# Hybrid attention block on one core: the attention weights turned by VectorE and DMA instead of TensorE, with the maximum, the scaling, the key order and the start-up rearranged

## The reference, cut to what matters

```python
h = rms_norm(x, norm_w)                       # x: 512 x 2048, fp32
proj = h @ w_in                               # 2048 x 6144
q, k, v, g_a, u_p, g_p = split(proj)          # 1024 columns each
# per head (8 heads, two components c of 64 each): q, k normed, rotary on 16 of 64
s = einsum('bhcqd,bhckd->bhcqk', q, k) / 8    # 512 keys
p = softmax(s)
a = p[:, :, 0] - lam * p[:, :, 1]             # differential attention
o = einsum('bhqk,bhke->bhqe', a, v)           # v: 512 keys x 128
attn = rms_norm(o, subln_w) * 0.8
pool = centred means of u_p over windows 2, 4, 8, 16, minus u_p, @ w_pool
x = x + concat(attn * silu(g_a), pool * silu(g_p)) @ w_out   # 2048 x 2048
```

## Time and profile before

| what | value |
|---|---|
| median of 3 runs | 777.97 us |
| the profiled execution | 778.13 us, span 776.3 us |
| PE busy | 769.8 us (99%) |
| PEld busy | 637.0 us (82%) |
| DVE busy | 551.0 us (71%) |
| ACT busy | 381.6 us (49%) |
| POOL busy | 31.3 us (4%) |
| chain that ended last | PE 96% |
| granted TensorE clock | 1.000 |

### The profile page before, as it was taken

The page is one execution under the profiler, slowest core; times in us unless marked ns, Lnnn a source line. Parts: engine busy times, 40 slices in busy tenths (PEclk is TensorE's granted clock), DMA queues, the critical chain, the costliest instruction groups (busy, mean ns, idle before and its releaser), DMA issues.

```text
span 776.3 us, 9638 instructions
## 1 busy us (share of the span) xinstructions
PE 769.8 (99%) x3458; PEld 637.0 (82%) x3458; DVE 551.0 (71%) x861; ACT 381.6 (49%) x649; POOL 31.3 (4%) x42
## 2 busy tenths in 40 slices
PE   9999999999999999999999999999999999999997
PEld 8788888888888888888888888888888888888886
DVE  5543235888854788985478897348888869987796
ACT  5463134444474354455354355554345665655552
POOL 0010000000000000000000000000000003322200
PEclk9999999999999999999999999999999999999999
DMA  9853323452222354221234421224432169999972
GB/s 333 327 194 92 98 89 102 135 156 70 74 73 64 109 149 126 78 81 55 81 110 147 122 81 57 79 78 139 140 105 81 56 233 255 276 275 263 211 168 108
DMA packets 67079, 106.22 MB, mean 137 GB/s; under 512 B 5344, under 2 KB 46560, under 8 KB 66528
## 3 DMA queue, kind: packets, MB, share of 16 engines
q1 hardware_dynamic: 60288, 86.72, 34.6%
q0 software_dynamic: 4736, 16.78, 11.0%
q10 hardware_dynamic: 2016, 2.18, 0.9%
HBM read 95.17 MB, written 4.19 MB: 128 GB/s over the span
## 4 chain that ended last, share of the span: by engine, by line
PE 96%; SPq 2%; DMA 1%; issue 0%; DVE 0%; ACT 0%
PE ps L457 94%; PE ps L584 2%; DMA raw<-in_w_in 1%; SPq L329 1%; SPq L286 1%; SPq L293 0%; SPq L331 0%; PE ps L625 0%; DVE x_left L1213 0%; ACT w_hi L675 0%
## 5 line engine op out<-in xcount | busy, mean ns | idle before, releaser
L903 DVE TENSOR_TENSOR w_lo<-raw,w_hi 128x512 fp32r<-128x512 f32 x240 | 163.4, 689 | 166.3 <-ACT w_hi L685 90.8
L457 PE MATMUL ps<-h_hi,w_hi 128*128 128x512 f32 x640 | 251.0, 392 | 0.0
L457 PE MATMUL ps<-h_lo,w_hi 128*128 128x512 f32 x640 | 249.3, 390 | 0.0
L457 PE MATMUL ps<-h_hi,w_lo 128*128 128x512 f32 x640 | 171.2, 389 | 0.0
L685 ACT CAST w_hi<-raw 128x512 fp32r<-128x512 f32 x149 | 90.6, 621 | 156.2 <-PE ps L457 155.4
L457 PEld LDWEIGHTS ps<-h_hi,w_lo 128*128 128x128 f32 x640 | 120.1, 188 | 25.1
L457 PEld LDWEIGHTS ps<-h_hi,w_hi 128*128 128x128 f32 x640 | 120.2, 188 | 24.6
L457 PEld LDWEIGHTS ps<-h_lo,w_hi 128*128 128x128 f32 x640 | 120.2, 188 | 24.5
L457 PE MATMUL ps<-w_hi,h_hi 128*128 128x512 f32 x352 | 122.0, 391 | 1.5 <-ACT w_hi L675 1.5
L457 PE MATMUL ps<-w_hi,h_lo 128*128 128x512 f32 x352 | 121.4, 389 | 0.0
L457 PE MATMUL ps<-w_lo,h_hi 128*128 128x512 f32 x352 | 121.4, 389 | 0.0
(11 more groups left out here) (143 smaller groups left out, 785.4 us busy)
## 6 DMA issues: line engine op xcount, KB each, us to landing
raw<-in_w_in SPq DMA_DIRECT2D x96, 512.0 KB, 3.7
raw<-in_w_out SPq DMA_DIRECT2D x12, 512.0 KB, 3.8
raw<-in_w_out POOLq DMA_DIRECT2D x12, 512.0 KB, 17.0
wide_b<-in_w_out POOLq DMA_DIRECT2D x12, 512.0 KB, 18.7
x_rows<-in_x SPq DMA_DIRECT2D x4, 1024.0 KB, 12.8
tall<-in_w_out SPq DMA_DIRECT2D x8, 512.0 KB, 13.1
tall<-in_w_out POOLq DMA_DIRECT2D x8, 512.0 KB, 23.4
mixed<-in_x_cols SPq DMA_DIRECT2D x3, 1024.0 KB, 13.2
```

What stands on the lines that cost most here:

```text
L457: last = nc.tensor.matmul(dst, lhs, rhs, start=first and i == 0, stop=final and i == len(pairs) - 1, skip_group_check=True)
L903: nc.vector.tensor_tensor(w_lo[:, slot, :], src, w_hi[:, slot, :].bitcast(F32), ALU.subtract).then_inc(w_lo_ready, 1)
```

## The change

What it does:
- The four TensorE transposes of each item are gone, and the identity with them. VectorE writes the difference of the two components to `at_raw`, without the scaling of component 0 (the coefficient is changed to fit). ScalarE multiplies `at_raw` in place by the reciprocal row sum. VectorE transposes it in 32 x 32 blocks into `turned`, and SP moves it by four DMAs of 64 KB back to `at_raw`, so that keys lie on partitions. ScalarE makes `at_hi` from it, VectorE `at_lo`.
- The keys of K are written in the order of their residue by 4, so that after the block transpose and the move each partition tile holds 128 successive keys. The product with v reads the queries in 16 runs of 32 (`key_tile`).
- All items come two steps earlier (scores in step 22+2i); `at_hi` of an item is made in step 28+2i, as before. The order of the second head's items and the places of the buffers change, so that the two heads' blocks overlap.
- VectorE's maximum is negated in one instruction and stands ahead of the weights' low part; the score's scale is folded into q's norm weight.
- VectorE's instructions of the first three rounds are written out instead of looped.
- The pool's mean is taken with a constant factor, and 8 columns at each edge are corrected, in place of a product with a full row.
- The epsilon row is spread by GpSimd. There are 9 warming products instead of 16. The first weight half is loaded by ScalarE's queue, x's first columns in smaller pieces, and the constants after the second reload of weights.
- In the output stage x's first block is loaded earlier and the last four blocks of the first wide pass later.

```diff
+        at_hi, _ = fixed("at_hi", [P, ST + 2, SEQ], F32R, at=at_hi_at)
+        at_lo, _ = fixed("at_lo", [P, ST + 2, SEQ], F32R, at=at_lo_at)
+        turned, _ = fixed("turned", [P, ST + 2, SEQ], at=at_hi_at)
+        at_raw, _ = fixed("at_raw", [P, ST + 2, SEQ], at=at_lo_at)
...
+        def item_place(i):
+            return (i, i) if i < ST else ((i + 2 - ST) % ST, (i + 2 - ST) % ST + 2)
...
-            load_x_cols(0, 0, 2)
-            load_v(0)
-            load_x_cols(1, 2, 4)
+            load_x_cols(0, 0, 1)
+            load_x_cols(1, 1, 2)
+            sp.dma_start(raw[:, 0, 512:1024], w_in_rows[:, 1, V_COLUMN:V_COLUMN + NC]).then_inc(raw_in[0], 16)
+            load_x_cols(2, 2, 4)
...
+            def move_item(rnd, i):
+                slot = item_place(i)[1]
+                sp.wait_ge(at_turned, rnd * ITEMS + i + 1)
+                for a in range(ST):
+                    sp.dma_start(at_raw[:, slot, a * P:(a + 1) * P],
+                                 turned[32 * a:32 * a + 32, slot, :]).then_inc(at_moved[i % 2], 16)
+
             def sp_round(r, last_round=False):
                 for unit in range(UNITS - G_UNITS if last_round else UNITS):
+                    if unit >= 10 and unit - 10 < ITEMS:
+                        move_item(r, unit - 10)
...
@@ pe_round @@
+            def key_tile(split, h, t):
+                slots = split[:, 2 * h:2 * h + ST, :]
+                return slots.rearrange("p s (a t i) -> p t s a i", a=ST, t=ST)[:, t].rearrange("p s a i -> p (s a) i")
-                    i, odd = divmod(m - 24, 2)
+                    i, odd = divmod(m - 22, 2)
...
-                        for t in range(ST):
-                            last = nc.tensor.transpose(ps[:, TB, t * P:(t + 1) * P],
-                                                       probs[:, 0, t * P:(t + 1) * P], ident[:, :])
-                        last.then_inc(at_transposed, 1)
...
@@ act_round @@
+                    i, odd = divmod(m - 24, 2)
+                    if 1 <= i <= ITEMS and not odd:
+                        slot = item_place(i - 1)[1]
+                        act.wait_ge(at_mixed, r * ITEMS + i)
+                        nc.scalar.activation(at_raw[:, slot, :], at_raw[:, slot, :], ACT.Copy, scale=row_inv[:, 0:1]
+                                             ).then_inc(at_scaled, 1)
+                    if 2 <= i < ITEMS + 2 and not odd:
+                        slot = item_place(i - 2)[1]
+                        act.wait_ge(at_moved[i % 2], r * (ITEMS // 2 * ST * 16) + ((i - 2) // 2 + 1) * ST * 16)
+                        nc.scalar.copy(at_hi[:, slot, :], at_raw[:, slot, :]).then_inc(at_hi_ready, 1)
+                    if 0 <= i < ITEMS and not odd:
+                        act.wait_ge(max_ready, r * ITEMS + i + 1)
...
@@ dve_round @@
                     if m == 16:
-                        nc.vector.tensor_tensor(wk(0), wk(2), wk(1), ALU.add).then_inc(qk_rotated, 1)
+                        nc.vector.tensor_tensor(wk(0).rearrange("p h (c j) -> p h j c", c=4),
+                                                wk(2).rearrange("p h (j c) -> p h j c", c=4),
+                                                wk(1).rearrange("p h (j c) -> p h j c", c=4), ALU.add
+                                                ).then_inc(qk_rotated, 1)
...
+                    if 1 <= i <= ITEMS and not odd:
+                        dve.wait_ge(at_scaled, r * ITEMS + i)
+                        slot = item_place(i - 1)[1]
+                        nc.vector.transpose(turned[:, slot, :], at_raw[:, slot, :]).then_inc(at_turned, 1)
...
-                    nc.tensor.matmul(ps[:, 0, :], ones_f32, eps_diag, start=True, stop=True).then_inc(eps_spread, 1)
...
-WARM = 16
+WARM = 9
```

More of the change, by code:

```diff
@@ L147, in hybrid_block @@
         coef = sb("coef", [P, 1])
+        edge = sb("edge", [P, N_WINDOWS, 2, PAD])
         ps = ctx.enter_context(nc.psum_tensor("ps", [P, 8, 512], F32))
@@ L190, in corner_part @@
             return corner[:, b % 2, (b // 2) * NC:(b // 2 + 1) * NC]
-        eps_diag, ones_f32 = probs[:, 0, :], gate[:, 0, 0:P]
-        rstd_line = head_out[0:1, :]
+        ones_f32 = gate[:, 0, 0:P]
+        rstd_line, eps_line = gate[0:1, 1, :], probs[0:1, 0, :]
         def wk(i):
@@ L425, in _ @@
             nc.gpsimd.memset(ones_f32, 1.0).then_inc(ones_set, 1)
+            pool.wait_ge(x_eps_ready, 1)
+            for t in range(ST):
+                pool.dma_start(eps_line[:, t * P:(t + 1) * P], x_eps[:, t:t + 1]).then_inc(eps_line_in, 16)
             pool.wait_ge(x_rstd_ready, 1)
@@ L594, in pe_round @@
                             lo = v_all[:, (KP + 2 * r + h) * SEQ + t * P:(KP + 2 * r + h) * SEQ + (t + 1) * P]
-                            last = products(ps[:, OB, :], [(hi, at_hi[:, t, :]), (hi, at_lo[:, t, :]),
-                                                           (lo, at_hi[:, t, :])], t == 0, t == ST - 1)
+                            last = products(ps[:, OB, :].rearrange("p (s n) -> p s n", s=ST),
+                                            [(hi, key_tile(at_hi, h, t)), (hi, key_tile(at_lo, h, t)),
+                                             (lo, key_tile(at_hi, h, t))], t == 0, t == ST - 1)
                         last.then_inc(head_done, 1)
@@ L809, in act_round @@
+                    if 0 <= i < ITEMS and not odd:
+                        act.wait_ge(max_ready, r * ITEMS + i + 1)
+                        for c in range(2):
+                            nc.scalar.activation(probs[:, c, :], ps[:, S0 + c, :], ACT.Exp,
+                                                 bias=neg_max[:, c:c + 1], scale=1.0,
+                                                 accum_out=row_sum[:, c:c + 1]).then_inc(exp_done, 1)
                     if m == 35:
@@ L846, in _ @@
             act.wait_ge(nw_in, 16)
-            for q in range(2):
-                x_high(q)
-                split_first(2 * q)
-                split_first(2 * q + 1)
+            for kk in range(2):
+                x_high(0, (kk,))
+                split_first(kk)
+            x_high(1)
+            split_first(2)
+            split_first(3)
             for n in range(1, HALVES):
@@ L880, in _ @@
         def _(dve):
-            steps = [0]
+            steps, chained = [0], [0]
             def setup(ins):
@@ L891, in _, with x_low @@
                 dve.sem_inc(started, START)
-            def x_low(q):
-                for kk in range(2):
+            def x_low(q, parts=(0, 1)):
+                for kk in parts:
                     k = 2 * q + kk
@@ L1121, in dve_round @@
                         split_form_low(2 * m - 77)
-                assert step[0] == STEPS, step[0]
             dve.wait_ge(nw_in, 16)
-            for q in range(2):
-                x_low(q)
-                for n in (2 * q, 2 * q + 1):
-                    split_rest(n, raw_half(n), n + 1)
+            for kk in range(2):
+                x_low(0, (kk,))
+                split_rest(kk, raw_half(kk), kk + 1)
+            x_low(1)
+            for n in (2, 3):
+                split_rest(n, raw_half(n), n + 1)
             for n in range(1, HALVES):
@@ L1172, in _ @@
                     v_low(n - 2 * KT - 1, 1)
-            with dve.Fori(0, ROUNDS - 1) as r:
+            for r in range(ROUNDS - 1):
                 dve_round(r)
```

235 lines of the change are left out of this document (106 added, 129 removed).

## The result

The kernel became slower: 787.17 us median (786.40 to 788.01, 4 runs) against 778.10 us before on the same chip (777.52 to 780.32, 4 runs), ratio 1.0116, 95% interval 1.0096 to 1.0136. The forecast was 777.5 us, no change.

A forecast was written before the change was run, and what follows sets the result against it. TensorE, busy 99% of the span, was taken to bound the kernel. From 778.13 us, savings of 19.2 and added costs of 18.8 gave 777.7, and with the median 0.2 lower 777.5 us, no change; range 768 to 788.

The forecast's parts named there:

- transposes and epsilon product gone: On TensorE, removing each item's four transposes saves 14.9 us and removing the epsilon product 0.9 us.
- first matmul earlier: At the start, TensorE's first real matmul comes at about 5.3 us in place of 7.31, saving 2.0 us.
- clock at the start: TensorE's clock when real work begins after nine warming products: no cost taken, up to 2 us if still slow.
- scores 3 to 6: Scaling and at_hi ahead of ScalarE's exponentials make these scores late, 0.85 us per item, four items a round.
- gate's read in step 40: VectorE's read of the GP gate's banks stands behind the block transpose: 0.9 us per round, +3.6 us.
- scores 0, q's move: A round's first scores come two steps earlier and lose their cover for q's move: 0 to 0.2 us per round, +0.3.
- Scores 1 have neither: The second scores of a round have neither scaling nor at_hi ahead of them on ScalarE, so no cost was booked.
- rival B: Slower: SP's move lands late and ScalarE stands at at_hi; 1.5 us late gives 789 us; chance 0.10.
- rival C: Runs of 32 columns slow TensorE's product with v, by up to 21.8 us, to 799 us; chance 0.05.
- K's add: VectorE's add writing K 512 bytes apart: between 1.22 us and twice that, taken as 1.22.
- A: Faster: the scores don't wait for ScalarE, 763 us, or 770 with half the late time; chance 0.15.
- D: Small unknowns go wrong (K's add, block transpose at its upper end, clock at the start): 780 to 784 us; chance 0.10.

The follow-up runs named there:

- Experiment 3: The changed kernel with a round's first maximum on VectorE ahead of the second head's q_low: 780.44 us, ratio 1.0040 to the kernel before the change.
- Experiment 11: The changed kernel with only SP's issue of the first head's q move put ahead of a weight load: 788.45 us.
- experiment 4: The changed kernel with 12 warming products in place of 9: 786.23 us, ratio 1.0107 to the kernel before the change.
- experiment 6: The changed kernel with K's keys in plain order and the product with v reading 512 successive columns: 784.10 us.
- kernel 1: The changed kernel with ScalarE's scaling and at_hi copy moved from its even to its odd steps: 770.08 us, ratio 0.9897 to the kernel before the change.
- experiment 9: The changed kernel with the at_hi copy behind the two exponentials of its own even step, not ahead of them: 778.91 us.
- experiment 2: The changed kernel with VectorE's read of the GP gate's banks ahead of the last block transpose in step 40: 785.24 us.
- experiment 8: The kernel before the change without TensorE's transposes in rounds 1 to 3, second head's sum of squares in the scores' bank: 769.34 us.
- kernel 7: The changed kernel with only the at_hi copy moved to ScalarE's odd steps, one step earlier: 796.19 us.
- kernel 10: The changed kernel with scaling and at_hi in odd steps, early first maximum, 12 warming products, and q's move issued ahead of a weight load: 763.55 us.
- kernel 5: The changed kernel with scaling and at_hi in ScalarE's odd steps, the first maximum ahead of q_low, and 12 warming products: 764.37 us.

## Why the prediction was wrong, point by point

Terms in us for the whole kernel; measured ones from the trace of after.

| step of the prediction | forecast | measured |
|---|---|---|
| transposes and epsilon product gone | -15.8 | -15.9 (with 0.91 for the epsilon) |
| first matmul earlier | -2.0 | -1.1 |
| wait at 29 gone | -1.4 | -1.4 |
| clock at the start | 0 (up to 2) | +1.5 |
| scores 3 to 6 | +13.6 | +12.4 |
| scores 2 | +1.3 | +1.0 |
| gate's read in step 40 | +3.6 | +3.1 |
| scores 0, q's move | +0.3 | +8.2 with scores 1 |
| scores 1 | 0 | (in that) |
| product with v in runs of 32 | 0 | +1.0 |
| small excesses of 0.02 to 0.04 in many steps | 0 | +1.2 |
| sum | -0.4 | +10.0, against 9.8 |

**The step that failed** is the sentence "Scores 1 have neither", with the +0.3 for "the scores two steps earlier" beside it. I had looked at what stands ahead of the exponential on ScalarE, found nothing for item 0, and booked nothing. What moved was the whole item, and its maximum then fell on VectorE into steps 22 and 23, where the second head's q_low and a delayed weight half are. Experiment 3 shows it: 2.06 us a round, of which 1.7 to 1.9 go with one instruction's place in the first three rounds, and 0.7 in the last. Experiment 11 shows that q's landing, the only thing that I priced there, takes nothing off the time of after when it alone is made early; it binds only once the maximum is early, for what then remains (0.2 to 0.4 us a round and 1.4 in the last). A step that is moved is moved on every engine, and on each the queue at its new place has to be read. That is 7.9 of the 10.2 us by which the sum missed. The measured 787.17 lies inside the range of 768 to 788 that the forecast left open, but only because the range went that far for rival B, and B is not what happened: that part is luck.

**The clock at the start** was named as an unknown of up to 2 us and taken as 0: +1.5 in this execution, and it shows in four of eight profiles with 9 warming products (experiment 4). The forecast had the rise after 4 us of work from one trace; it comes at 4.0 us in one trace and 6.6 in another with TensorE at work throughout, so that warming which ends at 5.2 is too short for some executions. **The first matmul** came at 6.19 and not 5.3, because ScalarE waited 0.90 us for the first weight half: its DMA was issued at 1.17 and landed at 5.40. I had counted only the norm's weights as the gate. **The runs of 32 columns** I took as free; they cost 11 ns a matmul (400 against 389), 1.0 us, and never approach rival C's 21.8.

**K's add** wrote 512 bytes apart at 2.06 us, near the upper end of my range, and not the 1.22 I took; the plain add of experiment 6 took the 1.22. The Trainium skill, "SBUF — State Buffer", section "Door 1: The DMA port swizzle", has a penalty for each access to a new line of 16 bytes, without a price. This add, where each 4-byte element falls on a new line, agrees with it: 1.69 times the plain one (2064 against 1218 ns). The block transpose took 711 ns (forecast 0.73, from the shuffle in the earlier trace rows). The estimate from the Trainium skill, "VectorE: DVE Perf Modes", section "The three transpose paths", was 1.24 us; the trace does not bear out that scaling, and the row of the nearest operation was the better guide.

**What was right.** The ScalarE chain is the main cost, with 3.11 us against 3.13, and it eats the gain of the transposes; experiments 1 and 9 show that it is the order and not the amount of work. The late time was 0.63 and not 0.75, since TensorE starts within 0.1 us of `exp_done` (195.56 to 195.60) where I had taken 0.14. The gate's read in step 40 was right in place and nearly in size (experiment 2). The removed transposes are worth 0.47 us where something else then bounds, but only 0.39 if nothing else is changed, since the scores have their own restart (experiment 8).

**The rivals.** A (the scores don't wait) is false for after and true for kernel 1. B does not occur in after, where the move has 0.5 us or more to spare in all but one item; ScalarE's waits for the moved tile appear in kernel 1 without cost, and in kernel 7, with the clock's falls behind them, they cost 9 us. C is false: the runs cost 1.0 us and not 21.8. D was named at 780 to 784 for three small unknowns: two of them did go wrong, the clock for 1.5 us and K's add for 0.44 x 4 = 1.8 (part of the 8.2).

**Left open:** no run here shows why TensorE's clock rises at 4.0 us in one execution and after 9 in another with the same start, nor why one wait among like ones is followed by a fall of the clock and the others are not.

## What to carry to other kernels

When an item is moved in a schedule, write down its neighbours on every engine at the new place, not only on the engine that was busiest before; the cost that was missed here came from the one whose queue was not read. If an engine feeds the bottleneck once per period and stands idle right before that (3.55 us here), what it must do for others belongs behind the release, not ahead of it: that order alone was 17 us. A DMA that somebody waits for is issued ahead of the bulk load that nobody needs yet; that was worth 0.8 us in kernel 10, and nothing where another queue bound (kernel 11).

## What the runs showed of the hardware

- TensorE's clock fell in the middle of a kernel. In kernel 11, after an idle time of 1.79 us, eight matmuls are 0.43 us apart in place of 0.23. A table by windows (us, then busy time of each engine, the granted clock, DMA share, GB/s) gives that stretch the lower of the two levels, 1.2 GHz in place of 2.4:

```profile
300.50:301.00 0.50, 0.50 (x3) 0.38 (x3) 0.47 (x2) 0.00 (x0) 0.00 (x0) 0.99 0.00 0
301.00:304.40 3.40, 3.40 (x9) 2.65 (x8) 2.16 (x3) 0.00 (x0) 0.00 (x0) 0.50 0.49 154
304.90:308.00 3.10, 3.10 (x14) 2.34 (x13) 1.64 (x3) 2.78 (x7) 0.00 (x0) 1.00 0.00 0
```

  The wait itself and the first six matmuls behind it (299.52 to 301.02) are still at full clock. It cost 1.6 us, once, where four such idle times stand in that trace. In kernel 7 three of four idle times of 2.6 to 3.7 us are followed by the same stretch of 3.4 us at half clock, 0.5 to 1.5 us after the matmuls resume. A wait of TensorE can cost more than its length.
- At the start of these kernels TensorE's clock rises at 4.0 to 6.6 us in nine traces, with TensorE at work, and at 9.4 to 10.0 in the four where the warming ended, at 5.2, with no fast product. In those four the first six or seven matmuls are 0.43 us apart. The listing gives 1.00 as their clock, but their traces have no record of it before the rise, so that the clock is the cause is inferred from the like distance and from the moment at which it ends.
- A move of 128 KB between partitions by SP lands in 2.2 us when nothing is ahead of it, and in up to 4.8 (after, 4.6 in kernel 5) with 512 KB of weights issued 1.5 us before.
- A TensorE operand read in runs of 32 fp32 columns costs 400 in place of 389 ns in the listing, a VectorE write with a stride of 512 bytes 2064 in place of 1218.
